# A 14,000-product kernel: one-column totals spread over the last tile, extra products at three boundaries, and a scaling moved up

## The reference

```python
for i in range(DEPTH):                                  # DEPTH = 2, D_MODEL = 1024, 272 tokens
    a_in = rms_norm(hs, norm_w[i, 0])
    mix = gated_deltanet(a_in, ...) if i % 2 == 0 else mlstm(a_in, ...)
    hs = hs + keep * rms_norm(mix, norm_w[i, 1])
    f = conv_ffn(rms_norm(hs, norm_w[i, 2]), ffn_w_up[i], ffn_conv_w[i], ffn_conv_b[i], ffn_w_down[i])
    hs = hs + keep * rms_norm(f, norm_w[i, 3])
# second block, l = 0, 1: proj = rms_norm(x) @ w_in; pooling, indexed attention with
# bias = rel_bias[rel_bucket(...)], memory attention (keys and values from mem @ w_mem_kv); gates; x + merged @ w_out
```

## Time and profile before

| | |
|---|---|
| median of three runs | 1634.6 us |
| the profiled execution: time, span | 1634.17 us, 1632.4 us |
| TensorE matmul busy | 1582.0 us (97%) |
| TensorE weight load busy | 1488.6 us (91%) |
| DVE, ACT, POOL busy | 1102.6, 944.8, 346.8 us |
| mean granted TensorE clock | 0.952 |

### The profile page before, as it was taken

How to read it: one execution, slowest core, us unless ns; L and a number is a source line. 1 busy time by engine, 2 the same in 40 slices (tenths; PEclk the granted TensorE clock), 3 DMA queues, 4 the chain that set the end, 5 groups by cost and what they waited for, 6 DMA issues and landing times.

```text
span 1632.4 us, 35024 instructions
## 1 busy us (share of the span) xinstructions
PE 1582.0 (97%) x14201; PEld 1488.6 (91%) x14201; DVE 1102.6 (68%) x2253; ACT 944.8 (58%) x1988; POOL 346.8 (21%) x412
## 2 busy tenths in 40 slices
PE   8998999999999999999999999999999989999998
PEld 6987987899899999987899999889999989899998
DVE  4776686558588864766689965667766666676663
ACT  6652664456376654546476754547676554667754
POOL 4231222133133322000423421003101210031010
PEclk9987797899799999999799999999999999999999
DMA  6320222035265554342346766545444645454452
GB/s 206 117 80 3 80 82 63 28 104 169 100 201 174 172 182 144 126 132 92 128 151 196 199 218 201 160 130 167 132 153 156 215 162 168 140 168 142 143 172 88
DMA packets 64976, 230.41 MB, mean 141 GB/s; under 512 B 7312, under 2 KB 9488, under 8 KB 64816
## 3 DMA queue, kind: packets, MB, share of 16 engines
q1 hardware_dynamic: 59792, 217.67, 42.3%
q0 software_dynamic: 4160, 8.98, 1.8%
q10 hardware_dynamic: 864, 1.52, 0.3%
HBM read 222.91 MB, written 5.24 MB: 140 GB/s over the span
## 4 chain that ended last, share of the span: by engine, by line
PE 77%; DVE 12%; ACT 5%; issue 3%; DMA 1%; POOL 1%; ACTq 0%; SPq 0%; DVEq 0%; POOLq 0%
PE ps L623 75%; DVE splitL L2305 4%; DVE arena L2313 3%; PE ps L627 3%; ACT splitH L1699 2%; ACT arena L1704 1%; DVE mixT L2310 1%; DVE arena L2310 1%; ACT L1704 1%; DVE arena L2321 1%; ACT sq L1704 1%; DMA ring<-wst 1%; POOL sq L3129 1%; ACT arenaR L1704 0%; DVE mixT L2313 0%
## 5 line engine op out<-in xcount | busy, mean ns | idle before, releaser
L2305 DVE TENSOR_TENSOR splitL<-ring,splitH 128x512 fp32r<-128x512 f32 x767 | 564.6, 765 | 244.0 <-ACT splitH L1699 235.5
L623 PE MATMUL ps<-aH,splitH 128*128 128x256 f32 (+2 forms) x2232 | 661.0, 297 | 13.4 <-DVE arena L2321 5.8
L623 PE MATMUL ps<-aH,splitL 128*128 128x256 f32 (+2 forms) x2232 | 640.5, 288 | 0.0
L623 PE MATMUL ps<-aL,splitH 128*128 128x256 f32 (+2 forms) x2232 | 626.8, 287 | 0.0
L1699 ACT ACTIVATE splitH<-ring 128x512 fp32r<-128x512 f32 x824 | 479.9, 622 | 130.5 <-PE ps L623 120.8
L623 PEld LDWEIGHTS ps<-aH,splitH 128*128 128x128 f32 x2232 | 429.8, 193 | 28.6 <-issue 11.5
L623 PEld LDWEIGHTS ps<-aH,splitL 128*128 128x128 f32 x2232 | 430.1, 193 | 0.0
L623 PEld LDWEIGHTS ps<-aL,splitH 128*128 128x128 f32 x2232 | 422.2, 192 | 0.4
L623 PE MATMUL ps<-arenaR,splitH 128*128 128x256 f32 (+2 forms) x1856 | 348.0, 288 | 3.0 <-POOL arenaR L3129 1.6
L623 PEld LDWEIGHTS ps<-arenaR,splitH 128*128 128x128 f32 x1856 | 290.9, 191 | 4.8 <-POOL arenaR L3129 1.9
L623 PE MATMUL ps<-arenaR,splitL 128*128 128x256 f32 (+2 forms) x928 | 264.2, 285 | 0.0
(11 more groups left out here) (212 smaller groups left out, 1282.5 us busy)
## 6 DMA issues: line engine op xcount, KB each, us to landing
ring<-wst SPq DMA_DIRECT2D x412, 512.0 KB, 3.9
mem_scratch<-arenaR POOLq DMA_DIRECT2D x16, 128.0 KB, 4.3
arenaR<-mem_scratch POOLq DMA_DIRECT2D x4, 512.0 KB, 8.2
rel_scratch<-arena POOLq DMA_DIRECT2D x8, 255.5 KB, 3.6
arena<-x SPq DMA_DIRECT2D x2, 512.0 KB, 4.9
arena<-mem POOLq DMA_DIRECT2D x2, 512.0 KB, 4.3
arena<-rel_scratch POOLq DMA_DIRECT2D x1, 1024.0 KB, 9.1
out<-arena ACTq DMA_DIRECT2D x4, 256.0 KB, 2.1
```

The lines of the kernel that those rows point to most:

```text
L623: return pe.matmul(out, lhsT, rhs, start=start, stop=stop)
L2305: dve.tensor_tensor(lo, raw, hi.bitcast(F32), ALU.subtract).then_inc(*inc(("lo_dve", q)))
```

## The change

It does five things. In `mix_sums` the six tallies of blocks `npq` and 6 are cut into twelve halves (two token groups each), one behind each step of the last tile from step 2, 4 or 0 on (K = 16, 22, 8; three halves per two steps for K = 8). In `add_norm` `warm` puts products that nobody reads (one column of ones against the 128x128 identity) where TensorE waits: 4, 1 and 6 of them, and 5 behind at the second and third boundary; `r1` is sent out before the `sb2` tally; banks are handed out and put back in another order; DVE does `scale(0)` ahead of the `u` chain and `scale(1)` behind `normed(0)`; ACT rounds pairs 0 and 1 before it copies the bias rows. In `second`, 8 and 10 unread products follow the `get` of the `ik` bank; three stand in the opening transposes. The bias products use 128 rows in place of 32, with zero rows written or loaded (the table becomes 128x512). 

```diff
+            def warm(b, n):
+                for _ in range(n):
+                    mm(psum[b][0:1, 384:512], ones[:, 0:1], ident)
+
+            def tally(out, src, n, part=None):
+                for q in range(GROUPS[n]) if part is None else range(part, GROUPS[n], 2):
...
+                def half(i):
+                    q, late = i // 2 % 3, i >= 6
+                    src, e = ((sq, "nsq"), (sc, "nsc"), (sb2, "nsb"))[q]
+                    if late:
+                        w.wait_ge(e, name, 6)
+                    else:
+                        w.wait_ge("npq", name, q, 5)
+                    tally(products(name)[q - 1] if q else psum[0][:, 0:4], src[:, 6 if late else 0], n, i % 2)
+
+                begin = {8: 0, 16: 2, 22: 4}[K]
-                        if m == 7 and k == 3:
+                        if m == 7 and k == begin:
...
-                            for q, src in enumerate((sq, sc, sb2)):
-                                w.wait_ge("npq", name, q, 5)
-                                tally(outs[q], src[:, 0], n)
-                            for q, (src, e) in enumerate(((sq, "nsq"), (sc, "nsc"), (sb2, "nsb"))):
-                                w.wait_ge(e, name, 6)
-                                tally(outs[q], src[:, 6], n)
+                        if m == 7 and begin <= k < begin + 12:
+                            if K == 8:
+                                for i in range(3 * k // 2, 3 * (k + 1) // 2):
+                                    half(i)
+                            else:
+                                half(k - begin)
@@ tensor, add_norm
+                Rb = bg.get("nRb", i)
+                warm(Rb, 4)
                 w.wait_ge("nsq", mix, 7)
                 tally(psum[0][:, 0:4], sq[:, 7], n)
                 frame(psum[0][:, 0:4], False).then_inc(*inc(("nS1", mix)))
...
+                w.wait_ge("nsc", mix, 7)
+                tally(products(mix)[0], sc[:, 7], n)
+                warm(Rb, 1)
+                rb = bg.get("nrb", mix)
                 w.wait_ge("tr1", mix)
+                tokens_out(rb, "r1", n).then_inc(*inc(("nrb", mix)))
+                w.wait_ge("nsb", mix, 7)
+                tally(products(mix)[1], sb2[:, 7], n)
+                frame(psum[s3][:, 0:8], False).then_inc(*inc(("nS3", mix)))
+                bg.put(s3, ("u", mix, 2))
+                warm(Rb, 6)
                 w.wait_ge("tr2", i)
+                tokens_out(Rb, "r2", n).then_inc(*inc(("nRb", i)))
                 if mix == "gdn":
                     for h in range(RELS):
                         biases(h)
+                else:
+                    b = bg.get("warm", mix)
+                    warm(b, 5)
+                    bg.put(b)
+                bg.put(rb, ("pmm", i, 3))
+                bg.put(Rb, ("nm", i, 3))
@@ tensor, second
                 b = fg.get("ik", l)
+                warm(b, 8 if l == 0 else 10)
@@ scalar, add_norm
+                highs(i, n, js=(0, 1))
                 if mix == "gdn":
                     for h in range(RELS):
                         biases(h)
-                highs(i, n)
+                highs(i, n, js=(2, 3))
@@ vector, add_norm
+                scale(0)
                 w.wait_ge("nS3", mix)
...
                 dve.reciprocal(tok("r2", n), tok("s2", n)).then_inc(*inc(("tr2", i)))
-                scale(0)
                 add(0)
+                normed(0)
                 scale(1)
-                normed(0)
                 add(1)
                 normed(1)
                 low(0)
@@ gpsimd, tables
+                pool.memset(relb, 0.0).then_inc(*inc(("rpad",)))
+                pool.dma_start(hot, arr["hot"]).then_inc(*inc(("rb", 0), by=16))
+                w.wait_ge("rpad")
+                pool.dma_start(relb[0:32, :], arr["rel_bias_2"]).then_inc(*inc(("rb",), by=16))
```

More of the change, by code:

```diff
@@ L740, in repay @@
                         bg.put(i, *fg.free[i])
-            def tally(out, src, n):
-                for q in range(GROUPS[n]):
+            def warm(b, n):
[3 more added lines that the diff above has]
+                for q in range(GROUPS[n]) if part is None else range(part, GROUPS[n], 2):
                     o, W_ = tile_of(q, n)
@@ L787, in biases @@
                 w.wait_ge("rcut")
-                mm(psum[b][:, :], relH[0:32, h:h + 1].broadcast_to([32, 128]), hotR[0:32, :], True, False)
-                mm(psum[b][:, :], relL[0:32, h:h + 1].broadcast_to([32, 128]), hotR[0:32, :], False, True).then_inc(*inc(("rel", h)))
+                mm(psum[b][:, :], relH[:, h:h + 1].broadcast_to([128, 128]), hotR, True, False)
+                mm(psum[b][:, :], relL[:, h:h + 1].broadcast_to([128, 128]), hotR, False, True).then_inc(*inc(("rel", h)))
                 bg.put(b, ("rrep", h))
             def add_norm(mix, i, n):
+                Rb = bg.get("nRb", i)
+                warm(Rb, 4)
                 w.wait_ge("nsq", mix, 7)
@@ L795, in add_norm @@
                 frame(psum[0][:, 0:4], False).then_inc(*inc(("nS1", mix)))
[L796 to L801, removed]
-                st0["free"] = [("ts1", mix)]
-                b = bg.get("nrb", mix)
-                w.wait_ge("tr1", mix)
-                tokens_out(b, "r1", n).then_inc(*inc(("nrb", mix)))
-                bg.put(b, ("pmm", i, 3))
-                b = bg.get("nRb", i)
+                st0["free"] = [("ts1", mix)]
+                s3 = bank["nS3", mix][0]
+                w.wait_ge("nsc", mix, 7)
+                tally(products(mix)[0], sc[:, 7], n)
+                warm(Rb, 1)
+                rb = bg.get("nrb", mix)
+                w.wait_ge("tr1", mix)
+                tokens_out(rb, "r1", n).then_inc(*inc(("nrb", mix)))
[4 more added lines that the diff above has]
+                warm(Rb, 6)
                 w.wait_ge("tr2", i)
-                tokens_out(b, "r2", n).then_inc(*inc(("nRb", i)))
-                bg.put(b, ("nm", i, 3))
+                tokens_out(Rb, "r2", n).then_inc(*inc(("nRb", i)))
                 if mix == "gdn":
@@ L1656, in main @@
                     bg.put(b, ("hs0", k))
+                    if k in (4, 7):
+                        warm(0, k // 3)
                     if k == 4:
@@ L1720, in scale, with highs @@
                 a(mixT[:, k, 0:n], hs[:, k, :], ACT.Copy, scale=V("norm_w" if i != "xn0" else "ng2", g + k)).then_inc(*inc(("sca", i, k)))
-            def highs(i, n, x=mixT):
-                for j in range(4):
+            def highs(i, n, x=mixT, js=range(4)):
+                for j in js:
                     s = slice(2 * j, 2 * j + 2)
@@ L2370, in add_norm @@
                 dve.reciprocal(r, tok("s1", n)).then_inc(*inc(("tr1", mix)))
[L2371 to L2381, removed]
                 rb, Rb = ps("nrb", mix)[:, 0:n], ps("nRb", i)[:, 0:n]
@@ L2401, in low @@
                     tt(pair(aL, j, n), pair(mixT, j, n), pair(aH, j, n).bitcast(F32), ALU.subtract).then_inc(*inc(("nlo", i, j)))
+                scale(0)
+                w.wait_ge("nS3", mix)
+                w.wait_ge("tr1", mix)
+                tt(u, S3[:, 0:q], r, ALU.mult).then_inc(*inc(("u", mix, 1)))
+                w.wait_ge("u", mix, 1)
+                stt(u, S3[:, 4:4 + q], 2.0, u, ALU.mult, ALU.add).then_inc(*inc(("u", mix, 2)))
+                w.wait_ge("u", mix, 2)
+                tt(u, u, r, ALU.mult).then_inc(*inc(("u", mix, 3)))
+                w.wait_ge("u", mix, 3)
+                tt(u, u, tok(ENERGY[mix][0], n), ALU.add).then_inc(*inc(("u", mix, 4)))
+                w.wait_ge("u", mix, 4)
+                ts(u, u, 0.0, ALU.max).then_inc(*inc(("tu", mix)))
                 w.wait_ge("ts2", i)
                 dve.reciprocal(tok("r2", n), tok("s2", n)).then_inc(*inc(("tr2", i)))
-                scale(0)
                 add(0)
+                normed(0)
                 scale(1)
-                normed(0)
                 add(1)
@@ L3527, in buckets @@
     bucket = np.where(rel > 0, 16, 0) + np.where(n < 8, n, large)
-    return ((np.arange(32)[:, None] == bucket[None, :]) * 1.0).astype(np.float32)
+    hot = np.zeros((128, 512), np.float32)
+    hot[:, 0:511] = np.arange(128)[:, None] == bucket[None, :]
+    return hot
 def vectors(a):
```

11 lines of the change are left out of this document (3 added, 8 removed).

## The result

The kernel after takes 1646.6 us (median, 1642.0 to 1649.1) against 1634.6 for the kernel before: ratio 1.0064, 95% interval 1.0038 to 1.0091. Slower, as forecast, but by 12.0 us (10.5 by the ratio) instead of 24. A second set of runs of the same kernel (`after_again`) gave 1652.9 against 1635.8, +17.1, ratio 1.0102 (1.0071 to 1.0134). By both, the change costs 10 to 17 us.

The account below looks back on a forecast made before the run. TensorE's own short work at a clock that may drop, and a serial chain behind the last tile, bind the boundaries. Boundaries 8.3, 7.0, 4.6 and `ik` 3.9 sum to 23.8 us on 1634.6, so 1658; range 1634 to 1664.

Parts of the forecast that it names:

- I take it that the clock falls about where it fell: First two boundaries' last tiles: clock falls 2.5 us behind the first frame, stays low; tiles end 4.8 and 5.5 us later.
- The term: Second boundary, last tile: with nine rounds and six steps, most at 1.2 GHz, it ends 5.5 us later.
- +7.0: Second boundary in all: 5.5 us for the tile plus 1.5 for the later lead behind it.
- Rival (2): The clock holds at one of the first two boundaries: +14 to 15 us, 1649; chance 0.12.
- The half: Last tile: each half between dense steps costs 0.52 us at 2.4 GHz and 0.78 at 1.2 GHz.
- Behind the tile at the first boundary: With the clock at 1.2 GHz from the tile on, 4.5 us later less 1.0 gained: 3.5 us.
- The bias product in the first lead: First boundary: the fourth bias row's product waits for a bank, leaving TensorE idle about 2 us, released by ACT.
- `r1` and a product ahead of `sb2`: Behind the last tile: both run ahead of the `sb2` tally, so the `u` chain starts 1.4 us later.
- Third boundary: At 1.2 GHz already; POOL's late sum, halves, unread products and `r1` make the lead 4.6 us later.
- `ik`: 8 and 10 unread products run behind the wait, when `ik` could: 1.75 + 2.2 = 3.9 us, nothing covering it.
- rival (4): Unread products before `ik` fill the wait and keep the clock: about -3 for +3.9, 1651; chance 0.06 with forecast's boundaries.
- Rival (1): Alternation, having dense work all along, holds the clock at the first two boundaries: +6.8 us, 1641; chance 0.20.

Follow-up runs that it names:

- e1_spread: The kernel before with the spread totals alone (twelve halves between dense steps, no unread products, old order behind the tile): 1639.3 us, ratio 1.0025.
- e2_addnorm: The kernel before with everything the change does behind the last tile, totals still in blocks: 1644.3 us, ratio 1.0053.
- e5_order: The kernel before with the change's new order behind the tile, without its unread products, totals in blocks: 1640.3 us, ratio 1.0038.
- e3_ik_behind: The kernel before with 8 and 10 unread products behind the claim of the `ik` bank, as in the change: 1639.1 us, ratio 1.0029.
- e7_frames_apart: The kernel before with the totals spread and their two frames behind two different dense steps, ahead of the first half: 1634.9 us, ratio 0.9995.
- e12_begin_swapped: The kernel before with the totals spread, the halves starting at step 4 at the first boundary and step 2 at the second: 1636.2 us, ratio 0.9997.
- e11_best_lead: The kernel before with totals spread, frames apart, unread products inside the `ik` wait and five in later lead waits: 1633.1 us, ratio 0.9979.
- e6_act: The kernel before with the one edit that ACT rounds the first two pairs ahead of the three bias copies: 1637.7 us, ratio 1.0019.
- e9_after_apart: The kernel after with the totals' two frames behind two different dense steps ahead of the first half: 1643.2 us, ratio 1.0052 against the kernel before.

## Why the prediction was right or wrong

Right in sign and in the places; wrong by a factor of two in size, above all because the clock was taken to fall at two boundaries and fell at one. Step by step:

- **The failed step: "I take it that the clock falls about where it fell", put to both boundaries.** At the first it did, in all executions of after and e1_spread. At the second it held through the tile in every execution with spread totals there (eleven, of nine kernels). The term was +5.5 us; it is -1.7. With that and the chain the second boundary is 0.0 to +2.8 in place of +7.0. Rival (2), the clock up at one of the two, was the one that happened; its 1649 lies between the medians of the two sets, 1646.6 and 1652.9. I gave it 0.12. Why the two boundaries differ the runs do not show; but a case of "both, one, or none" with an unknown cause should have had the middle as its likeliest.
- **The half: 0.52 and 0.78 us; measured 0.44 and 0.64.** I took the upper end because the nearest interleaved row had it. Twelve halves and the rounds at 1.2 GHz (1.46 for 1.32) make 1.5 us in the first boundary's tile (9 x 0.14 and 3 x 0.08). Measured there: the tile's square starts at 431.99 against 428.58, less the opening's 0.3: +3.1 in place of 4.8.
- **Behind the tile at the first boundary: 3.5; measured 0.6** (3.7 less 3.1). I had the clock at 1.2 GHz from the tile on. It came back at 433.1, 1.1 us behind the tile, and fell again at 436.5, for 10.3 us, as long as in before. Windows of after, of before and of e2_addnorm:

```profile
433.10:436.50 3.40, 3.40 (x32) 1.00 0.00 0
436.50:446.80 10.30, 10.30 (x43) 0.50 0.00 0
432.40:442.70 10.30, 8.89 (x31) 0.50 0.20 76
424.30:441.40 17.10, 17.10 (x68) 0.50 0.13 47
```

  So the same work met no more of the low clock than it had before. In e2_addnorm, with 6.8 us more of it, this stage is +4.3: the price was about right, the condition not.
- **The bias product in the first lead: an idle TensorE of about 2 us.** In after it is 0.68 us:

```profile
448.52 0.73 PE L623 MATMUL ps<-arenaR 128*128 128x512 f32 x2 [0.68 <-ACT arena L1731]
```

- **`r1` and a product ahead of `sb2`: 1.4 us.** Tile to `u` went from 3.3 to 5.1 us at 2.4 GHz, 1.8 in place of the 1.5 I had with the four products. The mechanism holds, and the order alone is +4.7 in the median over all three boundaries (e5_order).
- **Third boundary: 4.6; measured 5.1 and 4.6.** Right: POOL's late sum (796.10), four products before `sq`, `u` at 814.07 less 4.0, so 3.7 after 806.35 (forecast 4.2).
- **`ik`: 3.9; measured 2.2 and 5.0** in two executions of after, and +3.8 in the median of e3_ik_behind. That `warm` stands behind the wait and not in it was right, and rival (4) is refuted. What I left out is that the clock does not always fall there: a dip less or more is 1.5 us.
- **Rival (1)'s argument, that alternation holds the clock,** is right for most tiles (second boundary, e7_frames_apart, e12_begin_swapped). In e1_spread the clock fell without any idle time: 12.50 us busy of 12.50, and 0.62 of the clock. The rule of the Trainium skill weighed in the prediction (long idle gaps between bursts of matmuls lower the clock; page "TensorE: Matmul & The Clock Gate", section "HAM oscillation — how this bites in real kernels") does not account for that fall.

## What to carry to other kernels

Filler products helped here only inside a wait, and only at `ik` (five more in e11_best_lead's waits gave nothing): put them ahead of the instruction that carries the wait, on a bank that is free, and give them no more than the wait has at the lower clock. Short work spread between dense steps can keep the clock where a block of it loses it (the second boundary: eleven of eleven against none of six), but whether it does can hang on small things such as the place of two frames (the first boundary); try two or three placements and judge by a dozen runs each, since one profile of the same code differs from the next by more than the change is worth. When several edits share a stage, price them together: the work behind the tile was +9.0 us alone, and with the frames apart and the `ik` products inside their wait the whole change was level with the kernel before.

## What was not expected of the hardware

The same code ran its opening 11 us apart between two executions (-8.6 in e6_act, +2.8 in e5_order), with a mean granted clock of 0.91 and 0.88 in it. A full 12.5 us of uninterrupted TensorE work went at 0.64 of the clock (after_again) or at 1.00 (e9_after_apart) in kernels that differ only in the place of two frames of 0.3 us each. A clock that held in one place was not always kept: e7_frames_apart and e12_begin_swapped kept it through the first boundary's tile, then lost it behind the tile (0.53 in the window 430 to 431 of the latter), which kept -2 to -4 us from coming.
